# Six instead of four of the 22 tile pairs of a ConvFFN layer computed as seven block products

## The chip, the cores and the metric

The kernel runs on one core of a Trainium2 chip. The metric is the device time of one execution of the whole program, in microseconds (us); 1164.09 us is the median of three runs before the change, the lowest 1163.95 and the highest 1164.12.

The engines are named as in the profile: PE is TensorE (PEld its weight loads), DVE is VectorE, ACT is ScalarE, POOL is GpSimd, SP the engine that issues most DMAs.

## What is computed

A trunk of two layers over 576 tokens (512 of a prompt and 8 times 8 of samples). Each layer is a mixer and then a gated ConvFFN, which is where the change lies:

```python
h = rmsnorm(x, p["ffn_norm"][layer])
up = h @ p["w_up"][layer]                      # (tokens, 1024) @ (1024, 2 * 2816)
c, fb = causal_dwconv(up, ffn_bufs[layer], p["ffn_conv_w"][layer], p["ffn_conv_b"][layer])   # 3 taps
x = x + (jax.nn.silu(c[..., :D_FF]) * c[..., D_FF:]) @ p["w_down"][layer]                    # (2816, 1024)
```

## The kernel before

**Layout and precision.** Channels lie on the 128 partitions, the 576 tokens (T) along the free axis, in two halves of 288 (HALF). Every float32 product is made of three matmuls: each operand is split in a part `hi` (a copy of it in the type fp32r) and a part `lo` (what is left), and hi\*hi, lo\*hi and hi\*lo are added up in PSUM. So every weight tile that comes from memory (`raws`) costs ACT a copy (`w_hi`, signalled by `hi_ready`) and POOL a subtraction (`w_lo`, signalled by `lo_ready`). Weights lie in 4 buffers, used as 8 halves (`HALF_AT`).

**Up-projection.** The 2 x 2816 up channels of a layer are 22 pairs of 128-channel tiles; the first tile of a pair passes through silu and gates the second. GROUPS cuts the 22 pairs into groups of 6, 6, 6 and 4. PATTERN says of each pair how it is computed:

- `P`, plain: two units, one for each tile, of 8 channel blocks x 3 matmuls x 2 token halves = 48 matmuls, so 96 for a pair (line 594). ACT copies and POOL splits two tiles of 128x1024.
- `S`, seven block products (`pair_products`, line 870): the pair is seen as a 2x2 block product (upper and lower half of the 1024 input channels, first and second half of the tokens), and computed in the order `A11, S1, S2, A12, R3, R4, A22` with 7 x 4 x 3 = 84 matmuls. It needs sums of input blocks (`x_sums`, made once a layer during the first four pairs), four sums of weight blocks (S1, S2, R3 on POOL, line 1847, and R4 on DVE, line 2453), seven hi and seven lo parts of 128x512 (lines 1343 and 1854), and four copies of partial results out of their PSUM banks on ACT (`bank_copy`, line 1366), which later products or DVE sums build on. A product waits for the copy: S2 may start only when A11 has been copied into S2's bank (`pair_copy`), and that copy waits until the unit before has been evacuated from the bank (`acc_free`).

**After the up-projection of a pair**, DVE evacuates PSUM times the rms factor (`scaled_padded`, lines 2058 to 2065, for a unit; lines 2461 to 2487 for an S pair), ACT makes the first tap of the convolution (`tap0`, line 1420), DVE the other two (`taps`, line 2412), ACT the silu (line 1426), DVE the gated product (`gate_product`, line 2421, signalled by `h_ready`). In the first three groups the gated product is then cut into blocks for the down-projection: `blocks_hi` (ACT, lines 1393 to 1399), `blocks_lo` (DVE), and for the sums of blocks `block_sums_hi` (ACT, line 1407), `block_sums_lo` and `last_block_lo` (DVE, line 2291). For the first three pairs of a group this is little, for the last three it is some twenty operations.

**Down-projection.** After a group's up pairs come its down products: for the first three groups 28 block products of 9 matmuls (`block_products`, line 839, FAST), for the last one plain units. Products 0 and 1 of the 28 may start when the first unit of the pair before has left banks 0 and 1, products 2 and 3 when its second unit has left banks 2 and 3 (`acc_free` at `ud`).

**Order.** Every engine's program is written out by hand, without a scheduler. RUNS shifts the pairs by one: a group's run consists of its pairs without the first, then the next group's first pair, `(g+1, 0)`, whose evacuation (`ahead_evacuated`) and taps are pushed behind the last blocks of the own group, and then the 28 down products. `ahead_of` decides from PATTERN during which step of which pair ACT and POOL prepare which weights: a pair's own weights are prepared during the pair before. ACT waits in order: in the branch for `(g+1, 0)` its program is

```python
if h > g:
    weights_hi(layer, g, AHEAD[g][(h, i), 0])
    blocks_hi(nt - 1)
    block_sums_hi(nt - 1)
    weights_hi(layer, g, AHEAD[g][(h, i), 1])
    continue
```

and what `AHEAD` holds there depends on the kind of the pair before it:

```python
elif FAST[g]:
    steps[i, 0], steps[i, 1] = down(2, 3) if after_p else down(0, 1, 2, 3), down(4)
```

Down products 1 and 3 of a group need sums of weights that POOL makes (`block_sum`, lines 1821 to 1832; L1821 for these two).

Of the kernel before, what the change touches and what calls it, by code (L numbers as in the profile page):

```python
# [36 lines left out]
def hybrid_trunk(nc, x, params, w_in_ab, pool_w, w_out_ab, w_in_c, w_out_c, w_up, w_down, gate_w, gate_bias,  # L37
# [11 lines left out]
    KH = DH // P  # L49
    KF = w_down.shape[3] // P  # L50
    GROUPS = ((0, 6), (6, 6), (12, 6), (18, KF - 18))
    PATTERN = ("PPPPPP", "PPSPSP", "PPSPSP", "PPPP")
    PB = state_pool.shape[2]
    CB = state_conv.shape[2]
    TAPS = CB + 1
# [40 lines left out]
    for g, (_, n) in enumerate(GROUPS):  # L96
        RUNS.append([(g, i) for i in range(1 if g else 0, n)] + ([(g + 1, 0)] if g + 1 < len(GROUPS) else []))
    kind_of = lambda pair: PATTERN[pair[0]][pair[1]]
    U_PAIR, R_PAIR, U_DOWN, R_DOWN, PAIR_TURN, BEFORE = {}, {}, [], [], {}, {}
    units = raw_tiles = turns = 0  # L100
    for g, run in enumerate(RUNS):
        assert len(PATTERN[g]) == GROUPS[g][1] and kind_of(run[0]) == kind_of(run[-1]) == "P"
        for before, pair in zip([None] + run, run):
# [10 lines left out]
    pairs_hidden = lambda layer, g: layer * sum(FAST_PAIRS) + sum(FAST_PAIRS[:g])  # L114
    N_PAIRS = sum(kinds.count("S") for kinds in PATTERN)
    U_IN1 = U_FFN0 + N_FFN
# [157 lines left out]
    with ExitStack() as ctx:  # L274
# [1707 lines left out]
        def _(dve):  # L1982
# [298 lines left out]
            def ffn(layer):  # L2281
                n = 2 * layer + 1
                r = (2, 5)[layer]
                for g, (t0, nt) in enumerate(GROUPS):
# [157 lines left out]
                    def pair_weight_sum(i):  # L2442
# [4 lines left out]
                        if pair_turn(layer, g, i):  # L2447
                            before = [(l, h, a) for l in range(2) for h in range(len(GROUPS)) for a in range(GROUPS[h][1])
                                      if PATTERN[h][a] == "S" and (l, h, a) < (layer, g, i)][-1]
                            dve.wait_ge(lo_ready, U_FFN[before[0]] + U_PAIR[before[1:]] + PLACE["R4"] + 1)  # L2450
                        if g and PATTERN[g][:i].count("S") == 0:
                            dve.wait_ge(lo_ready, U_FFN[layer] + U_DOWN[g - 1] + MS)
# [353 lines left out]
```

## Time and profile before

| | |
|---|---|
| median of 3 runs | 1164.09 us (1163.95 to 1164.12) |
| the profiled execution's own time | 1163.62 us |
| its span | 1161.9 us |
| PE busy | 1145.3 us, 99% |
| POOL, DVE, ACT busy | 722.1, 818.0 and 580.0 us |
| granted clock | 1.00 from the first to the last slice but one |

The span is what lies between the first and the last instruction; the 1.7 us around it belong to the time too. PE's busy time is that of overlapping matmuls with modelled ends, so a busy PE says that PE never waited, not that it is at its peak.

### The profile page before, as it was taken

How to read it: one execution, taken by the hardware profiler on the slowest of the kernel's cores; microseconds unless marked ns; L12 is line 12 of the kernel's file. 1: busy time of each engine (PE TensorE's matmuls, PEld its weight loads, DVE VectorE, ACT ScalarE, POOL GpSimd, SP SyncE). 2: the span in 40 equal slices, each digit the busy share in tenths (PEclk: the TensorE clock that was granted, in tenths of full speed). 3: DMA queues.
4: the chain of work that ended last, by engine and by line, in shares of the span. 5: the costliest groups of instructions: out<-in, count | busy, mean ns of one | idle time of the engine just before them, and what ended most of it. 6: DMA issues, size and time to landing. Idle time of an engine off the chain costs nothing. (4 is left out here: it accounts for less than half of the span.)

```text
span 1161.9 us, 21843 instructions
## 1 busy us (share of the span) xinstructions
PE 1145.3 (99%) x8442; PEld 1124.9 (97%) x8442; DVE 818.0 (70%) x1506; ACT 580.0 (50%) x1113; POOL 722.1 (62%) x691
## 2 busy tenths in 40 slices
PE   8999999999999999999999999999999999999997
PEld 8887999999999999999999999999999999999997
DVE  5999768878677867775614644388686778678655
ACT  7475555544554555453613533366346545654543
POOL 3996344359867985872564324334698679768633
PEclk9999999999999999999999999999999999999999
DMA  6311242203421422131422222322042213232312
GB/s 233 117 56 36 67 146 81 93 28 95 142 65 44 149 73 92 56 137 51 149 84 91 69 69 74 117 82 65 28 147 91 80 61 116 74 92 80 120 51 82
DMA packets 35688, 104.01 MB, mean 90 GB/s; under 512 B 5105, under 2 KB 7153, under 8 KB 35569
## 3 DMA queue, kind: packets, MB, share of 16 engines
q1 hardware_dynamic: 31504, 98.92, 26.9%
q10 hardware_dynamic: 4080, 3.69, 1.1%
q8 instruction: 67, 1.10, 0.4%
q14 instruction: 37, 0.30, 0.1%
HBM read 98.29 MB, written 4.79 MB: 89 GB/s over the span
## 5 line engine op out<-in xcount | busy, mean ns | idle before, releaser
L594 PE MATMUL psum<-x_hi,w_hi 128*128 128x320 f32 (+2 forms) x1564 | 336.4, 297 | 1.3 <-POOL w_lo L1664 1.3
L594 PE MATMUL psum<-x_lo,w_hi 128*128 128x320 f32 (+2 forms) x1564 | 334.8, 295 | 0.0
L594 PE MATMUL psum<-x_hi,w_lo 128*128 128x320 f32 (+2 forms) x1564 | 334.1, 295 | 0.0
L1664 POOL TENSOR_TENSOR w_lo<-w_raw,w_hi 128x1024 fp32r<-128x1024 f32 (+1 forms) x84 | 181.8, 2169 | 188.0 <-ACT w_hi L1041 188.0
L594 PEld LDWEIGHTS psum<-x_hi,w_hi 128*128 128x128 f32 x1564 | 258.8, 188 | 3.6 <-POOL w_lo L1664 1.6
L594 PEld LDWEIGHTS psum<-x_hi,w_lo 128*128 128x128 f32 x1564 | 258.5, 188 | 0.0
L594 PEld LDWEIGHTS psum<-x_lo,w_hi 128*128 128x128 f32 x1564 | 257.3, 188 | 0.0
L2412 DVE SCALAR_TENSOR_TENSOR psum<-arena,params,psum 128x608 f32<-128x608 f32 x176 | 150.4, 854 | 58.8 <-ACT psum L1420 55.8
L1806 POOL TENSOR_TENSOR w_lo<-arena,w_hi 128x384 fp32r<-128x384 f32 x120 | 130.8, 1109 | 49.6 <-ACT w_hi L1331 49.6
L839 PE MATMUL psum<-block_hi,w_lo 128*128 128x288 f32 x504 | 149.2, 296 | 0.0
L839 PE MATMUL psum<-block_hi,w_hi 128*128 128x288 f32 x504 | 149.2, 296 | 0.0
L839 PE MATMUL psum<-block_lo,w_hi 128*128 128x288 f32 x504 | 149.1, 296 | 0.0
L1664 POOL TENSOR_TENSOR w_lo<-arena,w_hi 128x1024 fp32r<-128x1024 f32 (+1 forms) x49 | 111.4, 2290 | 47.5 <-ACT w_hi L1041 47.5
L1420 ACT ACTIVATE psum<-arena,params 128x608 f32<-128x608 f32 x88 | 75.9, 862 | 74.1 <-DVE arena L2065 57.4
L1041 ACT ACTIVATE w_hi<-w_raw 128x1024 fp32r<-128x1024 f32 (+1 forms) x84 | 78.2, 939 | 69.0 <-PE psum L594 48.8
L1331 ACT ACTIVATE w_hi<-arena 128x384 fp32r<-128x384 f32 x120 | 58.7, 518 | 87.7 <-DVE arena L2276 28.2
L839 PEld LDWEIGHTS psum<-block_hi,w_lo 128*128 128x128 f32 x504 | 95.0, 188 | 0.0
L839 PEld LDWEIGHTS psum<-block_lo,w_hi 128*128 128x128 f32 x504 | 94.9, 188 | 0.0
L839 PEld LDWEIGHTS psum<-block_hi,w_hi 128*128 128x128 f32 x504 | 94.9, 188 | 0.0
L2290 DVE TENSOR_TENSOR residual<-psum,residual 128x288 f32<-128x288 f32 x168 | 71.7, 452 | 22.4 <-ACT squares_sum L1370 12.9
L2291 DVE TENSOR_TENSOR block_lo<-psum,block_hi 128x288 fp32r<-128x288 f32 x144 | 56.6, 415 | 20.5 <-ACT block_hi L1397 7.9
L2058 DVE TENSOR_TENSOR arena<-psum,rstd 128x512 f32<-128x512 f32 x68 | 46.7, 687 | 31.5 <-PE psum L594 31.4
(270 smaller groups left out, 2207.1 us busy)
## 6 DMA issues: line engine op xcount, KB each, us to landing
w_raw<-in_w_up SPq DMA_DIRECT2D x44, 512.0 KB, 3.7
arena<-in_w_up SPq DMA_DIRECT2D x44, 512.0 KB, 4.3
arena<-in_w_down SPq DMA_DIRECT2D x24, 384.0 KB, 3.6
w_raw<-in_w_down SPq DMA_DIRECT2D x24, 384.0 KB, 3.2
w_raw<-in_w_in_c SPq DMA_DIRECT2D x16, 512.0 KB, 3.5
w_raw<-in_w_in_ab SPq DMA_DIRECT2D x11, 512.0 KB, 3.6
w_raw<-in_w_out_ab SPq DMA_DIRECT2D x16, 256.0 KB, 2.7
w_raw<-in_w_out_c SPq DMA_DIRECT2D x8, 512.0 KB, 3.6
```

Source lines behind the costliest of these rows:

```text
L594: last = nc.tensor.matmul(PS[:, 2 * (q % 2 if slot is None else slot) + half, 0:b - a], w[q][:, k * P:(k + 1) * P], r[:, r_at, a:b], start ...
L839: last = nc.tensor.matmul(PS[:, BANK[n], 0:HALF], ws[w][:, cols + k * P:cols + (k + 1) * P], rs[:, block, k, :], start=(k == 0 and a == 0) ...
L1041: nc.scalar.activation(w_hi[slot][:, 0:nk * P], raws[RAW_SLOT[raw]][:, 0:nk * P], ACT.Copy).then_inc(hi_ready, 1)
L1331: nc.scalar.activation(w_hi[HALF_AT[ud + n] // 2][:, at:at + nk * P], src, ACT.Copy).then_inc(hi_ready, 1)
L1420: nc.scalar.activation(conv_acc(j), window(j, 0), ACT.Identity, bias=pcol("ffn_conv_b", ti + layer * 2 * KF), scale=pcol("ffn_conv_w", ti ...
L1664: nc.gpsimd.tensor_tensor(w_lo[slot][:, 0:nk * P], raws[RAW_SLOT[RAW[u]]][:, 0:nk * P], w_hi[slot][:, 0:nk * P].bitcast(F32), ALU.subtract ...
L1806: nc.gpsimd.tensor_tensor(w_lo[w][:, at:at + nk * P], src, w_hi[w][:, at:at + nk * P].bitcast(F32), ALU.subtract).then_inc(lo_ready, 1)
L2058: nc.vector.tensor_tensor(halves(dst[:, pad:pad + PR]), PS[:, 2 * slot:2 * slot + 2, 0:cut], halves(rstd[:, 0:PR]), ALU.mult)
L2290: plus = lambda out, a, b: nc.vector.tensor_tensor(out, a, b, ALU.add)
L2291: minus = lambda out, a, b: nc.vector.tensor_tensor(out, a, b, ALU.subtract)
L2412: nc.vector.scalar_tensor_tensor(out=conv_acc(j), in0=window(j, k), scalar=pcol("ffn_conv_w", ti + (layer * FK + k) * 2 * KF), in1=conv_ac ...
```

## The change

One constant. The first group's sixth pair, (0, 5), and the last group's third pair, (3, 2), become `S`; nothing is written new, but all that `PATTERN` decides moves with it, in both layers.

```diff
     GROUPS = ((0, 6), (6, 6), (12, 6), (18, KF - 18))
-    PATTERN = ("PPPPPP", "PPSPSP", "PPSPSP", "PPPP")
+    PATTERN = ("PPPPPS", "PPSPSP", "PPSPSP", "PPSP")
     PB = state_pool.shape[2]
```

So the first group's run becomes P P P P S P (before: six P), the last group's P S P (before: three P); the runs of the two middle groups stay P S P S P P.

At three places the order of the engines matters for what follows. ACT, from the fifth to the sixth pair's end and the next group's first pair, in the program before (L1041 is a plain tile's hi part, L1331 that of a down product, L1397 to L1399 `blocks_hi`, L1420 a first tap, L1426 silu):

```order
L1426 ACTIVATE arena<-psum 128x608 [waits tap_ready]
L1331 ACTIVATE w_hi<-arena 128x384 [waits unit_done,raw_ready2]
L1331 ACTIVATE w_hi<-arena 128x384 [waits unit_done,w_sum_pool]
L1420 ACTIVATE psum<-arena,params 128x2x304 [waits pad_ready,acc_free]
L1331 ACTIVATE w_hi<-w_raw 128x384 [waits unit_done,raw_ready0]
L1331 ACTIVATE w_hi<-arena 128x384 [waits unit_done,w_sum_pool]
L1397 ACTIVATE block_hi<-psum 128x288 [waits h_ready]
```

and in the changed one, from the same silu (of the sixth pair) on:

```order
L1426 ACTIVATE arena<-psum 128x608 [waits tap_ready]
L1420 ACTIVATE psum<-arena,params 128x2x304 [waits pad_ready,acc_free]
L1331 ACTIVATE w_hi<-arena 128x384 [waits unit_done,raw_ready2]
L1331 ACTIVATE w_hi<-arena 128x384 [waits unit_done,w_sum_pool]
L1331 ACTIVATE w_hi<-w_raw 128x384 [waits unit_done,raw_ready0]
L1331 ACTIVATE w_hi<-arena 128x384 [waits unit_done,w_sum_pool]
L1397 ACTIVATE block_hi<-psum 128x288 [waits h_ready]
```

The hi parts of down products 0 and 1 have moved from before the second tile's first tap to behind it, so that all four stand in a row ahead of the sixth pair's blocks.

POOL, at the same place, before (L1821 is a sum of weights for down product 1 or 3, L1806 a down product's lo part, L1827 and L1830 further sums, L1887 and L1894 copies of state rows):

```order
L1821 TENSOR_TENSOR arena<-arena 128x384 [waits raw_ready3]
L1806 TENSOR_TENSOR w_lo<-arena,w_hi 128x384 [waits w_hi_ready] x2
L1821 TENSOR_TENSOR arena<-w_raw 128x384 [waits raw_ready1]
L1894 COPY arena<-arena 128x18 [waits acc_free]
L1887 COPY arena<-ffn_state_T 128x8x2 [waits tap_ready]
L1806 TENSOR_TENSOR w_lo<-w_raw,w_hi 128x384 [waits w_hi_ready]
```

and after:

```order
L1894 COPY arena<-arena 128x18 [waits acc_free] x2
L1887 COPY arena<-ffn_state_T 128x8x2 [waits tap_ready]
L1821 TENSOR_TENSOR arena<-arena 128x384 [waits raw_ready3]
L1806 TENSOR_TENSOR w_lo<-arena,w_hi 128x384 [waits w_hi_ready] x2
L1821 TENSOR_TENSOR arena<-w_raw 128x384 [waits raw_ready1]
L1806 TENSOR_TENSOR w_lo<-w_raw,w_hi 128x384 [waits w_hi_ready]
```

Before, the two copies stood between the sums and product 2's lo part, so the sums belonged to the sixth pair; now both sums belong to the next group's first pair.

DVE, at the end of the fifth pair of the first group, before (the last row of a pair's blocks, then the evacuation of its second unit):

```order
L2291 TENSOR_TENSOR block_lo<-psum,block_hi 128x288 [waits block_hi]
L2058 TENSOR_TENSOR arena<-psum,rstd 128x512 [waits unit_done,stash_ready]
L2065 TENSOR_TENSOR arena<-psum,rstd 128x8x8
L2412 SCALAR_TENSOR_TENSOR psum<-arena,params,psum 128x2x304 [waits tap0_ready]
```

and after:

```order
L2291 TENSOR_TENSOR block_lo<-psum,block_hi 128x288 [waits block_hi]
L2453 TENSOR_TENSOR arena<-arena 128x512 [waits raw_ready2,pair_sum_pool,stash_ready]
L2061 TENSOR_TENSOR arena<-psum,rstd 128x288 [waits unit_done]
L2062 TENSOR_TENSOR arena<-psum,rstd 128x224
L2065 TENSOR_TENSOR arena<-psum,rstd 128x8x8
L2412 SCALAR_TENSOR_TENSOR psum<-arena,params,psum 128x2x304 [waits tap0_ready]
```

The sum R4 now stands between the fifth pair's blocks and its evacuation.

## Rows read from the trace of the kernel before

**Rows 1.** The page's row of busy time, and its row of granted clock in 40 slices.
```profile
PE 1145.3 (99%) x8442; PEld 1124.9 (97%) x8442; DVE 818.0 (70%) x1506; ACT 580.0 (50%) x1113; POOL 722.1 (62%) x691
...
PEclk9999999999999999999999999999999999999999
```

**Rows 2.** PE's waits: what waited, for what, total us, times, longest.
```profile
PE psum L663 <- ACT x_hi L1051: 1.7, 1, 1.7
PE psum L594 <- DVE last_group_lo L2291: 1.5, 1, 1.5
```

**Rows 3.** The chain that ended last, second layer's ConvFFN: start, us, matmuls.
```profile
752.39 82.50 PE psum L594 x624
...
881.17 11.24 PE psum L870 x84
892.41 12.74 PE psum L594 x96
905.15 11.24 PE psum L870 x84
916.39 25.39 PE psum L594 x192
941.77 33.54 PE psum L839 x252
...
1082.19 38.09 PE psum L594 x288
```

**Rows 4.** Timeline of DVE (start, us), from the fifth to the sixth pair, first group.
```profile
809.46 0.45 DVE L2291 TENSOR_TENSOR block_lo<-psum,block_hi 128x288 fp32r<-128x288 f32 x1
809.83 0.68 DVE L2058 TENSOR_TENSOR arena<-psum,rstd 128x512 f32<-128x512 f32 x1
```

**Rows 5.** Timeline of DVE, second group, up to the S pair at 905.15.
```profile
902.50 0.76 DVE L2453 TENSOR_TENSOR arena<-arena,w_raw 128x512 f32<-128x512 f32 x1
905.19 0.46 DVE L2061 TENSOR_TENSOR arena<-psum,rstd 128x288 f32<-128x288 f32 x1 [1.93 <-PE psum L594]
```

**Rows 6.** Timeline of ACT in that S pair.
```profile
906.11 0.86 ACT L1420 ACTIVATE psum<-arena,params 128x608 f32<-128x608 f32 x1 [2.29 <-DVE arena L2065]
906.92 0.62 ACT L1343 ACTIVATE w_hi<-arena 128x512 fp32r<-128x512 f32 x1
907.44 0.39 ACT L1366 ACTIVATE psum<-psum 128x288 f32<-128x288 f32 x1
```

**Rows 7.** Timeline of PE's weight loads in that S pair, where product S2 begins.
```profile
908.06 0.19 PEld L870 LDWEIGHTS psum<-x_sums_hi,w_hi 128*128 128x128 f32 x1
```

**Rows 8.** Timeline of POOL, ACT and DVE behind that S pair, which ends at 916.39.
```profile
921.07 0.20 POOL L1887 COPY arena<-ffn_state_T 128x16 f32<-128x16 f32 x1 [2.33 <-DVE psum L2412]
...
922.41 2.00 ACT L1041 ACTIVATE w_hi<-w_raw 128x1024 fp32r<-128x1024 f32 x2
...
924.36 0.80 DVE L2421 TENSOR_TENSOR psum<-psum,arena 128x608 f32<-128x608 f32 x1
```

**Rows 9.** Timeline of ACT and POOL in the second group's last two pairs, 916.39 to 941.77.
```profile
931.95 0.93 ACT L1331 ACTIVATE w_hi<-arena 128x384 fp32r<-128x384 f32 x2
...
934.48 1.02 POOL L1821 TENSOR_TENSOR arena<-w_raw 128x384 f32<-128x384 f32 x1
...
935.53 0.53 ACT L1331 ACTIVATE w_hi<-arena 128x384 fp32r<-128x384 f32 x1 [1.45 <-POOL arena L1821]
936.36 0.41 ACT L1397 ACTIVATE block_hi<-psum 128x288 fp32r<-128x288 f32 x1 [0.30 <-DVE psum L2421]
```

**Rows 10.** Timeline of DVE and PE's weight loads at the second group's first down products.
```profile
941.47 0.19 PEld L839 LDWEIGHTS psum<-block_hi,w_hi 128*128 128x128 f32 x1
...
943.40 0.21 DVE L2065 TENSOR_TENSOR arena<-psum,rstd 128x64 f32<-128x64 f32 x1
...
943.88 0.19 PEld L839 LDWEIGHTS psum<-block_hi,w_hi 128*128 128x128 f32 x1
```

**Rows 11.** Timeline of POOL and PE's weight loads at the second group's 24th down product.
```profile
966.98 1.33 POOL L1806 TENSOR_TENSOR w_lo<-w_raw,w_hi 128x384 fp32r<-128x384 f32 x1
...
969.03 0.19 PEld L839 LDWEIGHTS psum<-block_hi,w_hi 128*128 128x128 f32 x1
```

**Rows 12.** Busy time of PE by stretch: stretch, us, busy (matmuls), clock, DMA share, GB/s.
```profile
1140.00:1155.00 15.00, 14.60 (x127) 1.00 0.16 67
1155.00:1161.90 6.90, 0.88 (x6) 0.72 0.58 200
```

**Rows 13.** Timeline of PE: matmuls of one shape at the start, early and late.
```profile
2.91 0.64 PE L703 MATMUL psum<-ones 128*128 128x128 f32 x2
...
4.19 0.87 PE L703 MATMUL psum<-ones 128*128 128x128 f32 x6
```

## What the change will do

> **What bounds the kernel now.** I read the page's busy times first: PE is busy 99% of the span at the full granted clock [rows 1]. Then PE's waits: the longest is 1.7 us, the next 1.5 us, and none lies inside the up- or down-projections [rows 2]. Then the chain of work that ended last: it is a string of PE pieces, stage behind stage without a gap [rows 3]. So a matmul taken out is worth its full pace, and a new wait of PE costs its full length. The question is only whether the new S pairs let PE run on as the four present ones do. In this chain a P pair takes 82.50 / 6.5 = 12.69 us (624 matmuls), an S pair 11.24 us (84 matmuls of 0.134), a P pair ahead of an S pair 12.74 us (its second unit is cut 288/288 instead of 256/320), and the 28 down products 33.54 us, 1.198 us each [rows 3].
>
> **The change part by part.**
>
> *Fewer matmuls.* Of each new S pair PE saves 12.69 - 11.24 = 1.45 us and the P pair ahead gives back 0.05, so 1.40 us; four new S pairs (two a layer, two layers): **-5.6 us**. This part has one answer: the chain is PE alone.
>
> *What S adds elsewhere.* Of an S pair POOL has 3 sums and 7 lo parts of 128x512 instead of two of 128x1024, ACT four bank copies, DVE one sum and more, shorter evacuations. In the second group this is hidden twice a layer: its two S pairs stand in the chain at exactly 11.24 us, with nothing between [rows 3]. But they stand in other surroundings than the new one of the first group, and there I find two places that are not covered.
>
> *Last group, pair (3, 2).* Its run P S P begins like that of the second group (P, S behind 28 down products), and its hidden tiles are cut in three pieces instead of into blocks, so ACT and DVE have less to do than there. Behind it comes a P pair whose evacuations find an idle DVE; the tail behind that is unchanged. Down weights 0 and 1 move into the last pair, four or five operations on POOL in 12.7 us. SP issues the same loads in the same order; those of down tiles 0 and 1 wait for lo parts of R4 and A22 and come later, but a pair ahead of their use. **0 us**, cover: the last P pair of 12.69 us; without it the down units would wait for hi and lo part, 1 to 3 us a layer.
>
> *First group, first place: the start of S pair (0, 5).* Product S2 needs A11's copy in its bank, the copy needs the evacuation of the unit before. In the second group the evacuation starts 0.04 us after the P pair has ended, at 905.19 [rows 5], the first tap follows at 906.11, R4's hi part at 906.92, the copy at 907.44, and it ends at 907.83 [rows 6]; S2's first weight load is at 908.06 [rows 7]: only 0.23 us to spare. There the P pair ahead has one of the light hidden tiles (index 0 or 2) to cut. Ahead of (0, 5) stands (0, 4) with hidden tile 3, a heavy one. The equal case before is the end of pair five, which by the chain is at 834.89 - 2 x 12.69 = 809.51 [rows 3]: there DVE's last block row starts at 809.46 and the evacuation at 809.83, 0.32 us after the end [rows 4]. Into this gap the change puts the sum R4 of 0.76 us [rows 5], which with the 0.1 us that DVE rows overlap moves the evacuation by 0.66 to 0.98 us after the end. That is 0.94 later than in the second group, and 0.23 of it is spare: **PE waits 0.7 us** ahead of S2. Bounds: 0 if the sum found room earlier (it can't, DVE works in order), and 0.7 + 0.76 = 1.5 if the sum took twice its time. I take 0.7; two layers, +1.4 us. What follows in this pair (copies, blocks of tile 4) was tied to PE by the copy of S2, and moves with PE.
>
> *First group, second place: from S(0, 5) over (1, 0) into the down products.* Nowhere in the kernel before do down products follow on S, P; it is always P, P. The nearest rows are the stretch behind the second group's S pair for what DVE and ACT still owe, and the second group's last pair for the down preparation. Let E be the end of the S pair (916.39 there). POOL's copy of state rows, in front of the sums, waits for taps and starts at E + 4.68 [rows 8]; the sum for product 1 is then ready at about E + 4.83 + 1.02 = E + 5.85. ACT is free for down hi parts where it now begins the next tiles' hi parts, E + 6.02 [rows 8]. From the first down hi part to the fourth it is 935.53 - 931.95 = 3.58 us, since the fourth waits for POOL's second sum, which waits behind the lo parts of products 0 and 1 [rows 9]. So ACT's fourth down hi part starts at E + 9.60, and `blocks_hi` of the sixth pair, queued behind it on ACT, 0.43 us later, at E + 10.03. Its input, the gated product, is there at 924.36 + 0.80, that is E + 8.77 [rows 8]: ACT's queue and not DVE sets the start. PE is at the first down product's weight load at E + 12.69 - 0.30 = E + 12.39 (weight loads run 0.30 ahead of matmul ends: 941.47 against 941.77) [rows 3, 10]. So `blocks_hi` starts 2.36 us ahead of the down products, where in the second group it starts 941.47 - 936.36 = 5.11 ahead [rows 9, 10]: 2.75 us later. All that hangs on it moves along, since it is one chain of ACT and DVE operations: B21, B22, T3, T2, T4, and behind T4 on DVE the evacuation of (1, 0)'s second unit. That evacuation ends at 943.40 + 0.21 = 943.61 in the second group, and the third down product, which needs it for bank 2, loads its first weights at 943.88 [rows 10]: 0.27 us to spare. **PE waits 2.75 - 0.27 = 2.5 us** ahead of the third down product of the first group; two layers, +5.0 us.
>
> *Is anything later still?* The lo parts of the down products follow the same hi parts. In the second group POOL's chain of lo parts passes through the whole stage with 969.03 - 968.31 = 0.72 us to spare at its tightest, product 23 [rows 11]. Moved by 2.75 us it would hold PE up by 2.03, which is less than the 2.5 that PE waits at the third product already: covered, by 0.45 us. The loads of the next down tiles wait for lo parts and move with them.
>
> Sum: -5.6 + 1.4 + 5.0 = **+0.8 us**. On the profiled execution's 1163.62 that gives 1164.4. The median of the runs shown is 0.5 us above it, so the forecast for the median is **1164.9 us**. Gain and losses all but cancel: the last group gains 2.8 us, the first loses 3.6.
>
> *A rule on the clock.* In the trace PE's clock stays at full rate, 2.4 GHz, through all waits, the longest of them 1.7 us [rows 2, 12], and falls only in the stretch from 1155, where almost no matmul is left [rows 12]. A wait of 2.5 us lies between, and no row of before shows what it does.
> The Trainium skill, "TensorE: Matmul & The Clock Gate" (Part 1: The HAM clock gate), says that an idle PE is put back to half its clock and needs sustained work to leave it. By that rule the two waits might each bring a slow stretch behind them and the sum would be the clock rival's, below; by the rows up to 1.7 us it is the sum above. I keep the sum.
>
> **The rivals.**
>
> *A. Neither wait comes, the cover holds.* For it: all four S pairs before run without a wait of PE, and the program keeps every rule of its order. Against it: the two spare times, 0.23 and 0.27 us, are smaller than what is added. Time: 1164.1 - 5.6 = 1158.5. Chance 0.07.
>
> *B. Half of the waits.* ACT and POOL could interleave faster than the rows of the second group tell (the sum for product 1 waits less, POOL's taps come earlier in a first group), so that `blocks_hi` starts some 1 to 1.5 us sooner: the down wait is 1 to 1.5 us, the sum -5.6 + 1.4 + 2.5 = -1.7: 1162.4, with 1161.0 at the end where the first wait is halved as well. Chance 0.15, a third of it under 1161.8.
>
> *C. Slower: POOL becomes the bound of the down stage.* POOL is busy through almost the whole stage. Its lo parts take 1.0 us alone but up to 1.33 [rows 11]; if four or five more of them than in the second group meet DVE's sums, the lo parts come 1.5 us later and the 0.45 us of cover are gone: PE waits 1 us more a layer, in small pieces from the ninth product on. It decides from 0.45 us of added lateness. Time: 1164.9 + 2.1 = 1167.0. Chance 0.14.
>
> *D. Slower: the clock falls in the wait.* At the start of the program two matmuls of a shape take 0.64 us, and six take 0.87 once the clock is up, so that one more costs 0.22 against 0.11 us [rows 13]; that stretch of about 3 us did in it what 1.5 us do later. One such stretch a layer: +3.0, 1167.9. Chance 0.04.
>
> **How the numbers follow.** The forecast has 0.60, with a range of its own of 1163.3 to 1166.6 (0.3 us either way on the first wait and 0.5 on the second, twice each, not all one way); A 0.07, B 0.15, C 0.14, D 0.04. A measurement of this kernel tells some 0.2%, 2.3 us, from no change: faster is below 1161.8, slower above 1166.4. Faster: A and a third of B, 0.12. Slower: D, two thirds of C and a tail of the forecast, 0.16. Same: 0.72. The range that leaves out no more than 2 in 10: 1161.6 to 1167.4.
>
> **What would show each step.** In the profile after, 8394 matmuls instead of 8442; in the chain of the first group an S pair of 84 matmuls between P pairs; a wait of PE of 0.7 us ahead of the third of its seven products, released by ACT's copy; a wait of 2.5 us at L839, released by DVE's evacuation L2065, once in each layer's first group and in none of the others; the last group shorter by 1.4 us without a wait. The prediction is wrong if PE's waits at L839 are released by POOL's lo parts (C), if none is there (A), if the waits are under 2 us (B), or if the granted clock dips behind them (D).

## The result: 1.1 us more, and the two waits where they were expected

The changed kernel takes 1165.03 us in the median of 17 runs (1164.35 to 1169.51), the kernel before 1163.95 (17 runs, 1163.46 to 1164.44). That is 1.1 us slower in the median and 2.0 us in the mean (1165.92 against 1163.93). The ratio, 1.0017 with an interval of 1.0010 to 1.0024, goes with the means: clear of 1, but inside the 0.2% that I called no change. The forecast was 1164.9, the range 1161.6 to 1167.4.

The profiled execution of the changed kernel took 1166.73 us (span 1165.0), so it is one of the longer runs, and the reason for that is a finding of its own, below. The page's busy times, and the first waits of PE in the order of their sum (what waited, for what, total us, times, longest):

```profile
PE 1144.1 (98%) x8394; PEld 1123.4 (96%) x8394; DVE 826.2 (71%) x1530; ACT 592.2 (51%) x1149; POOL 754.7 (65%) x723
```
```profile
PE psum L839 <- issue: 4.6, 2, 2.3
...
PE psum L870 <- ACT psum L1366: 0.9, 2, 0.4
```

There are 8394 matmuls, the number foretold, against 8442 [rows 1]. Two waits are new beside [rows 2]: one a layer at a down product (L839) and one a layer at a block product (L870). The chain of work that ended last, in the second layer's ConvFFN (start, us, matmuls), answers to [rows 3]:

```profile
753.72 50.78 PE psum L594 x384
...
814.53 8.24 PE psum L870 x60
822.76 12.69 PE psum L594 x96
835.46 2.40 PE psum L839 x18
837.85 2.31 issue
840.16 32.75 PE psum L839 x234
872.91 12.74 PE psum L594 x96
...
1086.67 12.74 PE psum L594 x96
1099.41 11.24 PE psum L870 x84
1110.64 12.71 PE psum L594 x96
```

The last group is 12.74 + 11.24 + 12.71 = 36.69 us instead of 38.09 [rows 3]: 1.40 saved, no wait. Before, the first group went from 752.39 to 868.43, 116.04 us. Now it goes from 753.72 to 872.91, 119.19 us: 3.15 more. That is 1.40 saved, and 4.55 lost at the two places below. For the whole program it is 2 x (3.15 - 1.40) = 3.5 us more in the two layers and 0.4 us less at the program's start, where PE leaves its wait at L663 at 8.91 us instead of 9.27: 3.1, which is what the spans differ by (1165.0 and 1161.9).

**First place, the start of S pair (0, 5).** Timeline of DVE (first fence), ACT (second) and PE's weight loads (third), start and us. The S pair's first weight load is at 810.59.

```profile
810.78 0.45 DVE L2291 TENSOR_TENSOR block_lo<-psum,block_hi 128x288 fp32r<-128x288 f32 x1
811.15 0.68 DVE L2453 TENSOR_TENSOR arena<-arena 128x512 f32<-128x512 f32 x1
811.75 0.45 DVE L2061 TENSOR_TENSOR arena<-psum,rstd 128x288 f32<-128x288 f32 x1
```
```profile
813.99 0.39 ACT L1366 ACTIVATE psum<-psum 128x288 f32<-128x288 f32 x1
```
```profile
814.50 0.19 PEld L870 LDWEIGHTS psum<-x_sums_hi,w_hi 128*128 128x128 f32 x1 [0.65 <-issue]
```

The sum R4 (L2453) stands between the last block row and the evacuation, which starts 0.85 us after the P pair's end (810.90) instead of 0.04 [rows 5]. A11's copy ends at 814.38, and S2's first load comes 3.91 us after the pair's first, where the four S pairs of the kernel before have 3.20 (908.06 - 904.86 in that of [rows 7]): **0.70 us lost** a layer. PE's wait is shown as 0.4 because the matmuls' modelled ends overlap the gap.

**Second place, the down products behind (1, 0).** POOL and ACT (first two fences), then DVE and PE's weight loads:

```profile
831.34 1.02 POOL L1821 TENSOR_TENSOR arena<-w_raw 128x384 f32<-128x384 f32 x1
```
```profile
828.79 0.93 ACT L1331 ACTIVATE w_hi<-arena 128x384 fp32r<-128x384 f32 x2
...
832.39 0.53 ACT L1331 ACTIVATE w_hi<-arena 128x384 fp32r<-128x384 f32 x1 [2.25 <-POOL arena L1821]
832.82 0.39 ACT L1397 ACTIVATE block_hi<-psum 128x288 fp32r<-128x288 f32 x1
```
```profile
838.87 0.46 DVE L2291 TENSOR_TENSOR block_lo<-psum,block_hi 128x288 fp32r<-128x288 f32 x1 [0.48 <-ACT block_hi L1407]
839.24 0.68 DVE L2058 TENSOR_TENSOR arena<-psum,rstd 128x512 f32<-128x512 f32 x1
839.84 0.21 DVE L2065 TENSOR_TENSOR arena<-psum,rstd 128x64 f32<-128x64 f32 x1
```
```profile
840.13 0.29 PEld L839 LDWEIGHTS psum<-block_hi,w_hi 128*128 128x128 f32 x1 [2.51 <-issue]
```

With E = 822.76, the first down hi part is at E + 6.03 (forecast 6.02), the fourth at E + 9.63 (9.60), `blocks_hi` at E + 10.06 (10.03), 2.33 us ahead of the first down product's load at 835.15. The evacuation ends at 840.05, and the third down product's load comes 0.08 later, 4.98 us after the first down product's. In the second group of the kernel before that distance is 943.88 - 941.47 = 2.41 [rows 10]. **2.5 us lost** a layer. The profile names no releaser ("issue"): that it is the evacuation follows from the order and the 0.08 us, and experiments below show it.

**What was not foretold: the clock.** Busy time of PE by stretch in the same execution (us, busy and matmuls, granted clock, DMA share, GB/s):

```profile
835.00:838.00 3.00, 2.85 (x22) 1.00 0.00 0
838.00:840.00 2.00, 0.00 (x0) 0.95 0.00 0
840.00:843.00 3.00, 2.84 (x12) 0.50 0.00 0
843.00:844.00 1.00, 1.00 (x8) 0.89 0.00 0
844.00:846.00 2.00, 2.00 (x17) 1.00 0.01 4
```

PE stood idle from 837.85 to 840.16, and at its end, from about 839.8 on (0.95 over 838 to 840), its clock was at 0.50, 1.2 GHz: from 840.16 to 843.17 it began 12 matmuls, at 0.240 us, where it needs 12 x 0.1335 = 1.60 us at full rate. **1.4 us lost**. With it the first group's account closes: -1.40 + 0.70 + 2.5 + 1.4 = +3.2. The first layer shows such a fall too, but later against its wait: there PE goes on at 261.83, runs 1.1 us at full rate, and then begins 14 matmuls at 0.240 us (262.98 to 266.33), which costs 1.5 us. The runs fall apart accordingly: nine of 17 with a mean clock of 0.998 or 0.999 lie between 1164.35 and 1165.03 (median 1164.6), two with 0.997 at 1165.86 and 1166.28, six with 0.995 or less from 1166.73 to 1169.51. Two falls put a run at 1164.6 + 2.9 = 1167.5, give or take the start; the longest, 1169.51, has the lowest clock of all, 0.994, which speaks for a third fall somewhere, not shown.
The Trainium skill, "TensorE: Matmul & The Clock Gate" (Part 1: The HAM clock gate), says that an idle PE is put back to half its clock, and that the count by which the clock is switched runs freely, so that the place of a switch varies from run to run (it shows this for the rise at a kernel's start). By that rule the split of the 17 runs would be expected. The trace agrees with the half rate (0.50), and with a place that is not tied to the wait: 0.4 us before PE goes on in the second layer, 1.1 us behind it in the first.

### The profile page after: what moved, and what is told of

Read it like the earlier page. It is cut to its first block and busy times, and to the rows that moved or that the text cites. A ratio compares the mean times of both kernels' runs of the same rounds, so it can differ in the third digit from the quotient of the medians.

```text
span 1165.0 us, 21906 instructions
## 1 busy us (share of the span) xinstructions
PE 1144.1 (98%) x8394; PEld 1123.4 (96%) x8394; DVE 826.2 (71%) x1530; ACT 592.2 (51%) x1149; POOL 754.7 (65%) x723
## 5 line engine op out<-in xcount | busy, mean ns | idle before, releaser
L594 PE MATMUL psum<-x_hi,w_hi 128*128 128x288 f32 (+2 forms) x1436 | 309.3, 297 | 1.3 <-POOL w_lo L1664 1.3
L594 PE MATMUL psum<-x_lo,w_hi 128*128 128x288 f32 (+2 forms) x1436 | 307.4, 295 | 0.0
L594 PE MATMUL psum<-x_hi,w_lo 128*128 128x288 f32 (+2 forms) x1436 | 306.9, 295 | 0.0
L1664 POOL TENSOR_TENSOR w_lo<-w_raw,w_hi 128x1024 fp32r<-128x1024 f32 (+1 forms) x80 | 172.2, 2158 | 163.9 <-ACT w_hi L1041 163.9
L594 PEld LDWEIGHTS psum<-x_hi,w_hi 128*128 128x128 f32 x1436 | 237.0, 188 | 3.6 <-POOL w_lo L1664 1.6
L594 PEld LDWEIGHTS psum<-x_hi,w_lo 128*128 128x128 f32 x1436 | 236.8, 188 | 0.0
L594 PEld LDWEIGHTS psum<-x_lo,w_hi 128*128 128x128 f32 x1436 | 235.8, 188 | 0.0
L1806 POOL TENSOR_TENSOR w_lo<-arena,w_hi 128x384 fp32r<-128x384 f32 x120 | 130.9, 1110 | 38.3 <-ACT w_hi L1331 38.3
L839 PE MATMUL psum<-block_hi,w_hi 128*128 128x288 f32 x504 | 150.7, 299 | 4.6 <-issue 4.6
L839 PE MATMUL psum<-block_hi,w_lo 128*128 128x288 f32 x504 | 150.6, 299 | 0.0
L839 PE MATMUL psum<-block_lo,w_hi 128*128 128x288 f32 x504 | 150.3, 298 | 0.0
L1664 POOL TENSOR_TENSOR w_lo<-arena,w_hi 128x1024 fp32r<-128x1024 f32 (+1 forms) x45 | 101.7, 2278 | 28.9 <-ACT w_hi L1041 28.9
L1420 ACT ACTIVATE psum<-arena,params 128x608 f32<-128x608 f32 x88 | 75.9, 863 | 68.6 <-DVE arena L2065 44.3
L1041 ACT ACTIVATE w_hi<-w_raw 128x1024 fp32r<-128x1024 f32 (+1 forms) x80 | 74.1, 934 | 71.3 <-PE psum L594 48.8
L1331 ACT ACTIVATE w_hi<-arena 128x384 fp32r<-128x384 f32 x120 | 58.7, 518 | 90.9 <-DVE arena L2276 29.5
L839 PEld LDWEIGHTS psum<-block_hi,w_hi 128*128 128x128 f32 x504 | 96.3, 191 | 5.0 <-issue 5.0
L839 PEld LDWEIGHTS psum<-block_lo,w_hi 128*128 128x128 f32 x504 | 96.2, 191 | 0.0
L839 PEld LDWEIGHTS psum<-block_hi,w_lo 128*128 128x128 f32 x504 | 96.2, 191 | 0.0
L1854 POOL TENSOR_TENSOR w_lo<-arena,w_hi 128x512 fp32r<-128x512 f32 x54 | 68.8, 1290 | 4.7 <-ACT w_hi L1343 4.7
```

What stands on the lines that cost most here:

```text
L594: last = nc.tensor.matmul(PS[:, 2 * (q % 2 if slot is None else slot) + half, 0:b - a], w[q][:, k * P:(k + 1) * P], r[:, r_at, a:b], start ...
L839: last = nc.tensor.matmul(PS[:, BANK[n], 0:HALF], ws[w][:, cols + k * P:cols + (k + 1) * P], rs[:, block, k, :], start=(k == 0 and a == 0) ...
L1041: nc.scalar.activation(w_hi[slot][:, 0:nk * P], raws[RAW_SLOT[raw]][:, 0:nk * P], ACT.Copy).then_inc(hi_ready, 1)
L1331: nc.scalar.activation(w_hi[HALF_AT[ud + n] // 2][:, at:at + nk * P], src, ACT.Copy).then_inc(hi_ready, 1)
L1420: nc.scalar.activation(conv_acc(j), window(j, 0), ACT.Identity, bias=pcol("ffn_conv_b", ti + layer * 2 * KF), scale=pcol("ffn_conv_w", ti ...
L1664: nc.gpsimd.tensor_tensor(w_lo[slot][:, 0:nk * P], raws[RAW_SLOT[RAW[u]]][:, 0:nk * P], w_hi[slot][:, 0:nk * P].bitcast(F32), ALU.subtract ...
```

## The experiments

The kernels of the last group alone, of the first group alone, of three moves and of the part made eight times ran on one chip (kernel before: 1163.89, 23 runs), the four others on another (1163.97, 19 runs). All of them compute the whole reference.

### The last group alone

Third pair of the last group S, as in the change; the first group left plain. To keep the number of S pairs even, as the layout of the weight halves demands, one S pair of the second group became P: S pairs in all as before the change.

```diff
-    PATTERN = ("PPPPPS", "PPSPSP", "PPSPSP", "PPSP")
+    PATTERN = ("PPPPPP", "PPSPPP", "PPSPSP", "PPSP")
```

> The last group's S pair alone, paid for with one S pair of the second group (the weight halves of a layer come out even only with an even number of S pairs): PATTERN PPPPPP, PPSPPP, PPSPSP, PPSP. My theory: an S pair in the last group is worth as much as one in a middle group, 1.40 us each, without a wait of PE, so the time is that of before within 0.3 us (1163.7 to 1164.3), and the last group's stage is 36.7 us instead of 38.1. The rival (something of the 1.1 us that the change lost was lost in the last group) expects 0.5 us or more above before and a wait of PE in that stage.

Measured: 1163.92 us, ratio 0.9998 (0.9989 to 1.0008). So an S pair is worth the same in the last group as in the second, and nothing is lost there. Nine of ten runs lie between 1163.65 and 1164.20. The tenth, 1166.09, is the profiled one. Here are its longest wait, at the program's start, and the clock by stretch behind it:

```profile
PE psum L663 <- ACT x_hi L1051: 2.2, 1, 2.2
```
```profile
11.80:14.80 3.00, 3.00 (x15) 0.50 0.70 251
```

That wait was 1.7 us in the profiled run of the kernel before, with no fall of the clock [rows 1, 2]. Behind 2.2 us one followed, 1.5 us after PE had gone on at 9.85, far from any part of the change.

### The first group alone

```diff
-    PATTERN = ("PPPPPS", "PPSPSP", "PPSPSP", "PPSP")
+    PATTERN = ("PPPPPS", "PPSPPP", "PPSPSP", "PPPP")
```

> The first group's S pair alone, paid for with one S pair of the second group: PATTERN PPPPPS, PPSPPP, PPSPSP, PPPP. My theory: all that was lost lies here. Against before: no matmul less in the sum, 2 x 0.7 us of waits ahead of S2, 2 x 2.5 us ahead of the third down product, so 1164.0 + 6.4 = 1170.4 at the full clock, and where the clock falls to half behind a wait of 2.3 us of idle PE, 1.4 us more each time: 1170.4 to 1173.2. The rival that puts a part of the loss into the last group expects less than 1169.5.

Measured: 1170.34, 1171.71, 1172.99 and 1173.54 us, with granted clocks of 0.999, 0.997, 0.996 and 0.995; ratio 1.0076 (1.0059 to 1.0093). The fastest is the profiled one. Its chain at the down products, and its clock by stretch:

```profile
837.68 2.40 PE psum L839 x18
840.07 2.29 issue
842.36 31.38 PE psum L839 x234
```
```profile
840.00:843.00 3.00, 0.71 (x6) 1.00 0.00 0
```

The same wait, and the clock stays up (column four): behind it 234 matmuls take 31.38 us, against 32.75 in the changed kernel's profile. With the number of S pairs that of before, both waits are all there is: 1163.9 + 2 x (0.70 + 2.5) = 1170.3, and 1170.34 was measured. Whether the clock falls is not fixed by the program.

### R4 behind the evacuation

In the first group alone DVE's sum R4 is moved behind the evacuation of the unit before.

```diff
-                        if following_s(g, (h, i)):
+                        if following_s(g, (h, i)) and g:
                             pair_weight_sum(i + 1)
                         scaled_padded(1, u + 1, up[:, 1, :], FB, tokens_cut(g, (h, i), 1))
+                        if following_s(g, (h, i)) and not g:
+                            pair_weight_sum(i + 1)
```

> The changed kernel with the first of the three moves alone: DVE makes the sum R4 for (0, 5) behind the evacuation of the unit before. If the 0.7 us ahead of S2 come from this sum, that wait shrinks to 0.1 us in both layers, and the wait of 2.3 us of idle PE ahead of the third down product stays as it is with its dips of the clock: without a dip 1164.4 - 1.2 = 1163.2, with two up to 1166.2. The rival (the copy is late for another reason, say ACT's own queue) expects the wait at S2 unchanged and 1164.4 at least.

Measured: median 1165.77 us, ratio 1.0012 (1.0002 to 1.0021). The two of ten runs at clock 0.998 or 0.999 took 1163.20 and 1163.59; three at 0.997 took 1164.72 to 1165.22, five at 0.995 or 0.996 took 1166.33 to 1166.74. Eight of ten runs have a clock that tells of a fall, so the median says little of the move; the two fastest runs and the profile say more. In the profile the wait at L870 is gone:

```profile
811.33 11.28 PE psum L870 x84
```

S2's load comes 3.30 us after the pair's first instead of 3.91: 0.60 of the 0.70 us are back. The last 0.10 I put down to the block row that still stands ahead of the evacuation, as in [rows 4]; no run shows it apart. The wait at L839 stays 2.3. Without a fall of the clock the sum gives 1163.95 - 5.6 + 0.2 + 5.0 = 1163.6.

### Three down hi parts instead of four ahead of the blocks

ACT's fourth down hi part, the one that waits for POOL's second sum, goes behind `blocks_hi`.

```diff
-                            weights_hi(layer, g, AHEAD[g][(h, i), 0])
+                            ahead = AHEAD[g][(h, i), 0]
+                            weights_hi(layer, g, ahead[:3])
                             blocks_hi(nt - 1)
+                            weights_hi(layer, g, ahead[3:])
```

> The changed kernel with the second move alone: ACT makes the fourth down hi part behind blocks_hi of the sixth pair. If ACT's queue set the start of blocks_hi, this starts 3.6 us ahead of the down products instead of 2.35, when DVE's gated product is there, and the wait ahead of the third down product shrinks by that 1.25 us, to 1.2 to 1.3 us: 1164.4 - 2.5 = 1161.9 at the full clock. A wait of that length let the clock stay up in all eight runs with the delayed DVE, so the runs should lie within 0.6 us and the granted clock at 0.998. If the chain behind blocks_hi is bound by something else, the wait stays 2.3 us of idle PE.

Measured: 1162.40 us, ratio 0.9990 (0.9980 to 0.9999). PE's wait there:

```profile
PE psum L839 <- issue: 2.2, 2, 1.1
```
```profile
829.79 0.41 ACT L1397 ACTIVATE block_hi<-psum 128x288 fp32r<-128x288 f32 x1 [1.45 <-DVE psum L2423]
```

`blocks_hi` now starts 3.56 us ahead of the down products instead of 2.33: it waits for DVE's gated product, as in the kernel before. The evacuation ends 1.2 us sooner and PE's wait shrinks from 2.3 to 1.1, so 1.2 us a layer of the loss were nothing but the place in ACT's queue. The chain of its stage is still 1.33 us longer than in the kernel before, and its profile shows no fall of the clock. Eight of ten runs lie under 1162.9; the others took 1163.71 (clock 0.997) and 1164.00 (0.998).

### All three moves

To these two moves a third is added: DVE evacuates (1, 0)'s second unit between T2's and T4's lo parts, no longer behind T4's (T2 and T4 are two of the sums of blocks of the gated product).

```diff
                         minus(bl[:, T2, k, :], front, f32(bh, T2, k)).then_inc(blk_ready, 1)
+                        if between is not None:
+                            between()
 ...
-                        block_sums_lo(nt - 1)
+                        block_sums_lo(nt - 1, (lambda: ahead_evacuated(1)) if g == 0 else None)
                         last_block_lo(nt - 1)
-                        ahead_evacuated(1)
+                        if not (g == 0):
+                            ahead_evacuated(1)
```

> The changed kernel with three moves in the first group alone: DVE makes the sum R4 for (0, 5) behind the evacuation of the unit before instead of ahead of it; ACT makes the fourth down hi part behind blocks_hi of the sixth pair instead of ahead of it; DVE evacuates the second unit of (1, 0) between T2's lo part and T4 instead of behind T4. My theory: both waits go (0 to 0.1 us left ahead of S2, none ahead of the third down product), with them every dip of the clock: 1164.0 - 5.6 + 0.1 = 1158.5, with all runs within 0.5 us of each other and the granted clock 0.998. The rival (POOL's lo parts become the bound of the down stage as soon as the evacuation is not) expects waits of PE at L839 released by L1806 and 1160 to 1162.

Measured: 1161.73 us (ten runs, 1161.33 to 1162.14), ratio 0.9981 (0.9972 to 0.9991). This missed 1158.5 by 3.2 us. The wait that was to go is gone, but another has come in its place:

```profile
PE psum L839 <- POOL w_lo L1808: 1.2, 4, 0.4
```

Timeline of ACT, then of POOL, then of PE's weight loads:

```profile
834.92 0.41 ACT L1407 ACTIVATE block_hi<-psum 128x288 fp32r<-128x288 f32 x1 [2.19 <-DVE psum L2293]
835.23 0.52 ACT L1331 ACTIVATE w_hi<-arena 128x384 fp32r<-128x384 f32 x1
```
```profile
835.83 1.01 POOL L1808 TENSOR_TENSOR w_lo<-arena,w_hi 128x384 fp32r<-128x384 f32 x1 [2.08 <-ACT w_hi L1331]
```
```profile
838.97 0.19 PEld L839 LDWEIGHTS psum<-block_hi,w_hi 128*128 128x128 f32 x1 [0.62 <-POOL w_lo L1808]
...
843.05 0.19 PEld L839 LDWEIGHTS psum<-block_hi,w_hi 128*128 128x128 f32 x1 [0.45 <-POOL w_lo L1808]
```

POOL stands idle for 2.08 us because the fifth down product's hi part (835.23) is queued on ACT behind T4's (834.92), which waits for DVE's block sums. From the sixth product on the lo parts come too late for PE: PE waits for them at the sixth, the ninth and, for under 0.1 us each, the tenth and eleventh product. From the first down product to the second group's first S pair it is 880.64 - 832.59 = 48.05 us, where the next kernel has 46.28: 1.77 us a layer. This is rival C's mechanism (PE released by POOL's lo parts), and the rival of the expectation above, which named 1160 to 1162. The next kernel shows that its cause lay on ACT, not in POOL's pace.

### All three moves, and the fifth hi part early as well

```diff
+                            if g == 0:
+                                weights_hi(layer, g, ahead[first:])
                             block_sums_hi(nt - 1)
-                            weights_hi(layer, g, AHEAD[g][(h, i), 1])
+                            if g:
+                                weights_hi(layer, g, ahead[first:])
```

Here `first` is 3 in the first group, and `ahead` holds all five down hi parts.

> The kernel with all three moves, and a fourth: ACT makes the hi part of the fifth down product right behind the fourth, ahead of the hi parts of the block sums, so that POOL's chain of lo parts starts some 2 us earlier. The three moves alone left PE 1.46 us of waits a layer in the first group's down stage, released by POOL's lo parts. If that chain was late because its first link, the fifth hi part, stood behind T4 on ACT, the waits at L839 go altogether: 1161.7 - 2.9 = 1158.8. If POOL is simply too busy in this stage after an S pair, whatever the start, it stays above 1160.5.

Measured: 1158.27 us (1158.13, 1158.21, 1158.33 and 1160.47), ratio 0.9958 (0.9941 to 0.9974): **5.7 us faster than the kernel before**, and the fastest of all. ACT, POOL and the chain:

```profile
827.91 0.94 ACT L1331 ACTIVATE w_hi<-arena 128x384 fp32r<-128x384 f32 x2
```
```profile
832.12 1.01 POOL L1811 TENSOR_TENSOR w_lo<-arena,w_hi 128x384 fp32r<-128x384 f32 x1
```
```profile
807.01 11.28 PE psum L870 x84
818.29 12.69 PE psum L594 x96
830.98 33.54 PE psum L839 x252
864.52 12.74 PE psum L594 x96
```

The fourth and fifth hi parts run at 827.91, and POOL's lo part of the fifth product starts at 832.12, 1.44 us behind the first down product's load instead of 3.5. The first group's down products take 33.54 us without a gap, as before the change. All that is left of the two losses is 0.1 us a layer at S2.

### The wait without the change

Does the length of the wait at L839 alone bring the fall of the clock? Both kernels start from the one before the change, with four S pairs. In the first group DVE makes T4's lo part eight or ten times, each time waiting for the last; the values stay the same.

```diff
+                            for _ in range(again):
+                                held_times[0] += 1
+                                minus(bl[:, T4, k, :], front, f32(bh, T4, k)).then_inc(held, 1)
+                                dve.wait_ge(held, held_times[0])
                             minus(bl[:, T4, k, :], front, f32(bh, T4, k)).then_inc(blk_ready, 1)
 ...
-                        last_block_lo(nt - 1)
+                        last_block_lo(nt - 1, 0 if g else 7)
```

> The kernel before, without any new S pair, with T4's lo part of the first group made eight times instead of once, each behind the one before, so that DVE reaches the evacuation of (1, 0)'s second unit some 3.5 us later; 1.2 us of it are spare, so PE waits 2.3 us ahead of the third down product in each layer. If a wait of this length alone lets the clock fall, without S pairs or anything else of the change, the granted clock dips behind it in a part of the runs, by 1.4 us each time: 1164.0 + 4.6 = 1168.6 without a dip, up to 1171.4 with two, and the runs lie several us apart. If the dips come from the S pair's stage, all runs lie within 0.5 us at about 1168.6 and the clock stays at 0.998.

Measured with eight: 1166.99 us, ratio 1.0027 (1.0017 to 1.0038), the granted clock 0.998 or 0.999 in all eight runs. The wait came out at 1.36 us, not 2.3:

```profile
835.45 3.90 DVE L2292 TENSOR_TENSOR block_lo<-psum,block_hi 128x288 fp32r<-128x288 f32 x8 [0.48 <-ACT block_hi L1408]
```
```profile
840.20:843.00 2.80, 2.80 (x21) 1.00 0.00 0
```

The seven repetitions add 3.44 us, but the evacuation moves by 2.7 only: in this place of the kernel before it does not wait for DVE, it waits until PE has ended the unit (it ends 1.24 us behind the first down product's load, that is 0.30 for PE's end and 0.9 for itself). So the first 0.7 us were free; I had not counted that. So I made the part ten times:

```diff
-                        last_block_lo(nt - 1)
+                        last_block_lo(nt - 1, 0 if g else 9)
```

> The kernel before with T4's lo part made ten times, which holds the evacuation of (1, 0)'s second unit back so that PE waits about 2.3 us ahead of the third down product (seven extra ones gave 1.5, idle PE 1.36 us, and no dip of the clock in 16 waits). Theory that the length of the wait alone decides: 1163.9 + 4.7 = 1168.6 without a dip and runs that lie up to 3 us above, with a granted clock of 0.995 to 0.997 in them. Rival that the dips need something of the S pair's stage: all runs at 1168.6 within 0.6 us and 0.998.

Measured: 1169.99, 1170.51, 1171.84 and 1171.98 us, with clocks of 0.996, 0.997, 0.995 and 0.995; ratio 1.0065 (1.0048 to 1.0082). PE's waits, and the clock in the second layer:

```profile
PE psum L840 <- issue: 4.7, 2, 2.3
```
```profile
839.40:841.70 2.30, 0.01 (x1) 1.00 0.00 0
842.40:844.80 2.40, 2.40 (x11) 0.50 0.00 0
```

One microsecond more of the same wait, no S pair added, and all four runs have a mean clock of 0.997 or less. In the profile the clock fell 0.7 us after PE had gone on again. In the first layer of this execution the wait is as long (2.34 us) and no fall follows it. That execution is the one of 1169.99; without its fall of 1.5 us it would stand at 1168.5, as expected. The two longest runs lie 1.9 us above it, which fits one fall more; of those no profile is there.

## Why the prediction was right, step by step

**Fewer matmuls, -5.6: right.** An S pair in the chain is 11.24 us, the last group is shorter by 1.40, and the kernel with every wait removed is 5.7 us faster.

**Last group, 0: right.** By the chain, and by the last group alone (0.9998). One reading on the way was wrong: that none of PE's waits lies inside the up- or down-projections [rows 2]. L594 is the plain units' line, and its 1.5 us, released by `last_group_lo`, lies in the last group's down-projection of the first layer; another of 0.9 us lies at the same place in the second. Both are in the changed kernel's profile at the same length, so the sum was not touched.

**First place, 0.7: right.** 0.70 by the loads, and R4 moved gives 0.60 of it back. Two small errors cancelled in it. The evacuation started 0.85 us behind the pair's end, 0.81 later than in the second group, where the sum took 0.94. And not all of the 0.23 us to spare were to be had: S2's load came 0.12 us after the copy's end (814.38 to 814.50; 0.11 us in the kernel with R4 moved), the least that a run here shows, so 0.11 were spare, and 0.81 - 0.11 = 0.70. The 1.5 us bound did not come near.

**Second place, 2.5: right in size and cause.** Every time on the way (first and fourth hi part, `blocks_hi`) came within 0.03 us, since each was taken as a distance from the S pair's end in the same kind of stretch. Taking the fourth hi part out of ACT's way gave back 1.2 us of PE's wait, the third move the rest. The releaser that I named, L2065, is not what the profile prints.

**Lo parts covered, 0: right for the changed kernel, and the cover was real.** POOL's lo parts release none of PE's waits there. In the kernel with three moves, where the wait at the third product is gone, they bound the stage by 1.77 us a layer. I had put this at 2.03 us without the cover, for the 24th product; it came, but from the sixth to the eleventh product.

**The clock: the weak step, and by the prediction's own sign a wrong one.** A dip of the granted clock behind the waits was named as what would show the forecast wrong and D right, and it is there behind both waits of the profiled execution. I kept the sum by the waits up to 1.7 us, which have no fall [rows 2, 12], and gave rival D 0.04. In 8 of 17 runs at least one of the two waits brought a fall. The reasoning failed in that one wait that leaves the clock up says nothing certain of another, longer by 0.8 us: the kernels show the same 2.3 us with and without a fall. Its price was right (foretold 1.5 us a fall, measured 1.4 and 1.5). That the forecast of 1164.9 meets the median, 1165.03, so closely is luck: nine of 17 runs have no fall, with 1164.6 as their median, and the median of all 17 is the slowest of these nine. The next run is at 1165.86; one more run with a fall, and the median would have been there or higher, still inside the range. D should have had about as much as the forecast itself. Rival A and rival B did not come: the waits have their full length in every profile of the unmended change.

The single terms add up in the other kernels too: 1163.95 - 5.6 + 1.4 + 2 x 1.33 = 1162.4 for the ACT move (its stage of down products is 1.33 us longer than in the kernel before), and 1162.40 was measured; 1163.95 - 5.6 + 0.2 + 2 x 1.77 = 1162.1 for the three moves, and 1161.73 was measured.

**Still open.** Five runs of kernels without a 2.3 us wait at the down products lie 1.3 to 2.2 us above their fellows. That of the last group alone has its fall at the program's start in its profile. Of the others there is no profile: one of the kernel before (1165.77, clock 0.997), one with the ACT move (1163.71, 0.997) and the one with the fifth hi part early (1160.47, 0.996) have a low mean clock, so a fall at the start is likely for them, not shown; the other with the ACT move (1164.00) has 0.998, as runs without a fall have, and stays unexplained. What decides whether a 2.3 us wait lowers the clock was not tried.

## What to carry to other kernels

An operation that gains the same 1.4 us wherever PE is the bound can lose 3 us by its neighbours: look, for each new place, at what stands in each engine's queue between a producer and the buffer that PE needs next, and measure the distances in a stretch of the same kind. An operation that waits for another engine (here one hi part of 0.5 us, waiting for POOL) must not stand ahead of a chain on the way to PE, and when it is moved, look at once at what was hidden behind the same wait. Where PE would stand idle for more than 2 us, put the slow stretch behind it into the sum. In the profiles here it followed five of eight such waits (two each of the change, of the first group alone, of R4 moved and of the part made ten times).

## What the runs showed of the hardware

- PE's clock can fall to 1.2 GHz after an idle of 2.2 to 2.3 us, in some executions and not in others: of the four kernels with two waits of 2.3 us, 8 of 17, 3 of 4, 8 of 10 and 4 of 4 runs have a mean clock of 0.997 or less. Of the 32 runs of the four kernels whose longest wait at the down products is 1.36 us or less, 30 have 0.998 or more.
- A fall costs 1.4 to 1.5 us: twelve to fourteen matmuls of 288 columns at 0.240 us instead of 0.1335.
- It need not begin while PE is idle: in three profiles matmuls went on at full rate for 0.7 us (the part made ten times), 1.1 us (the change, first layer) and 1.5 us (the last group alone, at the start) and then fell to half.
